# Matrix memory of a hybrid decoder: sample tokens by heads on partition groups, spreads and state updates in split parts

## What is computed

```
F = cumsum(fc);  Dlog = F[t] - F[s] + i[s] (s <= t);  inter = m + F
m_t = max(max_s Dlog, inter);  W = exp(Dlog - m_t);  g = exp(inter - m_t)
S = (q k^T) * W
num = S v + g * (q C);   den = sum(S) + g * (q n)
h = num / max(|den|, exp(-m_t))
C_new = gC * C + sum_s wk[s] k[s] v[s]^T     (wk, gC: from the chunk's last token)
n_new = gC * n + sum_s wk[s] k[s]
```

## Time and profile before

| | |
|---|---|
| median of 3 runs | 1681.45 us |
| the profiled execution, its own time | 1674.11 us |
| its span, first to last instruction | 1672.0 us |
| TensorE busy | 1590.9 us (95%) |
| VectorE, ScalarE, POOL busy | 779.8 (47%), 464.9 (28%), 415.9 (25%) |
| granted TensorE clock, mean | 0.983 |
| chain that ended last | TensorE 52%: L1623 30%, L1601 15%, L1404 6% |

### The profile page before, as it was taken

One profiled execution on the slowest core, in us unless ns is written; L12 is line 12 of the kernel. 1 busy time (PEld: TensorE's weight loads), 2 busy tenths in 40 slices (PEclk: granted clock), 3 DMA queues, 4 the chain that ended last, 5 costly groups with the idle time before them and its releaser, 6 DMA issues.

```text
span 1672.0 us, 27426 instructions
## 1 busy us (share of the span) xinstructions
PE 1590.9 (95%) x10756; PEld 1472.2 (88%) x10756; DVE 779.8 (47%) x1682; ACT 464.9 (28%) x948; POOL 415.9 (25%) x388
## 2 busy tenths in 40 slices
PE   6999999999999998789999999999999999999984
PEld 6986799999996665578789999999999999999983
DVE  2008599999816652454554313223133231332347
ACT  3336523212226562253252111111111111111013
POOL 3520155222200001115394112221122211222004
PEclk8999999999999998999999999999999999999997
DMA  5220231133216107024202111101111011110002
GB/s 168 59 60 15 64 99 56 52 95 98 70 48 232 34 20 228 27 78 159 76 1 76 51 51 51 52 26 51 52 51 51 27 51 51 51 51 26 26 1 104
DMA packets 116781, 110.38 MB, mean 66 GB/s; under 512 B 15906, under 2 KB 101542, under 8 KB 116658
## 3 DMA queue, kind: packets, MB, share of 16 engines
q1 hardware_dynamic: 116658, 108.61, 20.7%
HBM read 88.61 MB, written 19.95 MB: 65 GB/s over the span
## 4 chain that ended last, share of the span: by engine, by line
PE 52%; DVE 2%; issue 1%; ACT 0%; DVEq 0%
PE bank L1623 30%; PE bank L1601 15%; PE bank L1404 6%; DVE y_tm L1835 1%; DVE stats L1810 1%; PE bank L1544 0%; DVE y_tm L1838 0%; PE bank L1767 0%; DVE y_acc L1609 0%; PE bank L1031 0%; PE bank L1000 0%; PE bank L1038 0%; ACT y_tm L1785 0%; DVE moments L1816 0%; DVE moments L1827 0%
## 5 line engine op out<-in xcount | busy, mean ns | idle before, releaser
L1623 PE MATMUL bank<-x_split,gate_up_split 128*128 128x352 f32 x3168 | 510.8, 323 | 2.8 <-issue 1.5
L1623 PEld LDWEIGHTS bank<-x_split,gate_up_split 128*128 128x128 f32 x3168 | 507.3, 188 | 3.7 <-issue 2.1
L2082 PE MATMUL bank<-w_split,xT_split 128*128 128x256 f32 (+1 forms) x2160 | 273.8, 285 | 8.4 <-POOL w_split L2288 8.0
L2082 PEld LDWEIGHTS bank<-w_split,xT_split 128*128 128x128 f32 (+1 forms) x2160 | 258.9, 181 | 14.5 <-issue 9.1
L1601 PE MATMUL bank<-hidden_split,weight_split 128*128 128x352 f32 x1584 | 258.6, 324 | 9.0 <-DVE y_acc L1609 6.9
L1601 PEld LDWEIGHTS bank<-hidden_split,weight_split 128*128 128x128 f32 x1584 | 255.6, 189 | 10.2 <-DVE y_acc L1609 7.8
L1694 DVE TENSOR_TENSOR hidden<-silu,bank 128x352 f32<-128x352 f32 x66 | 34.4, 522 | 413.0 <-ACT silu L1664 412.9
L1729 POOL TENSOR_TENSOR gate_up_split<-gate_up,gate_up_split 128x2048 fp32r<-128x2048 f32 x22 | 104.3, 4739 | 379.0 <-ACT gate_up_split L1656 379.0
L1609 DVE TENSOR_TENSOR y_acc<-y_acc,bank 128x352 f32<-128x352 f32 x264 | 137.3, 521 | 108.9 <-PE bank L1601 107.6
L2380 DVE TENSOR_SCALAR_CACHE_REDUCE chosen<-scores,level 128x384 uint8<-128x384 f32 (+2 forms) x198 | 174.3, 942 | 1.2
L2140 PE MATMUL bank<-xT_split,w_split 128*128 128x352 f32 x864 | 138.8, 323 | 1.2 <-ACT feature_stage L2253 1.2
(11 more groups left out here) (256 smaller groups left out, 1586.0 us busy)
## 6 DMA issues: line engine op xcount, KB each, us to landing
w_unit<-in_w_in_dram SPq DMA_DIRECT2D x16, 1024.0 KB, 5.6
gate_up<-in_w_gate_dram SPq DMA_DIRECT2D x22, 512.0 KB, 4.0
gate_up<-in_w_up_dram SPq DMA_DIRECT2D x22, 512.0 KB, 5.3
down_weight<-in_w_down_dram SPq DMA_DIRECT2D x11, 1024.0 KB, 4.9
scratch_dram<-feature_stage SPq DMA_DIRECT2D x36, 176.0 KB, 1.9
scores<-in_x_prompt_dram SPq DMA_DIRECT2D x8, 512.0 KB, 5.2
out_dram<-stage SPq DMA_DIRECT2D x32, 128.0 KB, 1.7
out_weight<-in_w_out_dram SPq DMA_DIRECT2D x16, 256.0 KB, 6.4
```

The costliest lines, as they stand in the source:

```text
L1623: mm = pe.matmul(PS[2 * c + w][:, 0:CH], gs[u][:, a, w, k, :], xs[:, b, k, c * CH:(c + 1) * CH], start=(k == 0 and (a, b) == PARTS[0]), st ...
L2082: mm = pe.matmul(bank[0:rows(i), 0:HALF], xs1[:, a, k, tile_cols(i)], w[:, b, k, :], start=(k == 0 and (a, b) == PARTS[0]), stop=(k == KD ...
```

## The change

- *Split rows.* Both rows of the spreads are kept as high and low parts in f32r: ScalarE rounds (`act_rows_high`, first thing in its sample attention), POOL subtracts (`pool_rows_low`), SP sends both parts onto partitions 4 to 11 beside the row itself (`sp_samples`, four DMAs), and VectorE casts the three parts to f32r (`dve_rows_round`, ahead of `norm(0)`). A spread is then one f32r matmul. Copies of `head_row` and of the sample mask are loaded early, five DMAs ahead of `load_w(3)`.
- *Heads on partition groups.* In chunk 0 head h has partitions 32h to 32h + 31: scores, weights, `weigh`, outputs, denominator and turning back handle one tile for all four heads; the output matmuls go to four column groups by `tile_position`, sequence by sequence. The wait for the state load (`c_in`) moves from `act_columns` to `sample_outputs`.
- *Split sample updates.* Keys (weighted, three parts on 96 partitions) and values (unweighted, three parts) are f32r; the pieces go to banks 6, 6 and 7.
- *Decay by POOL.* POOL multiplies a head's states by their decays (`scale`); VectorE adds the bank in three sums (`carry_samples`).
- Loads of the sample values: three parts (`mv3`) and one by head (`mvs`).

The core of the diff:

```diff
+            for part in (1, 2):
+                sp.dma_start(head_row[MH * part:MH * part + MH], c_rows[:, T:T + MH * P].rearrange("q (h n) -> q h n", h=MH))\
+                    .then_inc(rows_split, 16)
+            for part in range(1, MH):
+                sp.dma_start(new_mask_t[SMP * part:SMP * part + SMP, :], c_small[0:SMP, 96:128]).then_inc(rows_split, 16)
...
+            sp.wait_ge(pool_made, ROWS_LOW)
+            for w in range(2):
+                for part, src in ((1, rows_high), (2, rows_low)):
+                    sp.dma_start(row_parts[w][MH * part:MH * part + MH, :], src[:, w, :].bitcast(F32)).then_inc(rows_split, 16)
             sp.wait_ge(smp_kT, PAGES * EARLY)
...
+            for h in range(MH):
+                sp.dma_start(mvs[SMP * h:SMP * h + SMP, 0:P], mv_dram[SEQ:T, P * h:P * h + P]).then_inc(c_in, 16)
             for h in range(MH):
                 sp.dma_start(cn[:, h, :, 0:P], state_C[0, :, h].rearrange("b d e -> d b e")).then_inc(c_in, 16)
...
+        def act_rows_high(act):
+            act.wait_ge(rows_split, 16 * 5)
+            act.activation(head2[:, 0:MH, :], head_row, ACT.Copy)
...
+            for w, row in enumerate((b_row, g_row)):
+                act.activation(rows_high[:, w, :], row, ACT.Copy).then_inc(row_act, 1)
+
+        def dve_rows_round(dve):
+            dve.wait_ge(rows_split, 16 * 9)
+            for w in range(2):
+                dve.tensor_copy(row_split[w], row_parts[w]).then_inc(row_step, 1)
...
+            act.wait_ge(mv_loaded, 16 * (LAST + 3))
+            act.activation(v3[0:R3], mv3[0:R3], ACT.Copy).then_inc(sample_split, 1)
+            act.wait_ge(smp_values, 1)
             act.wait_ge(a_turned, 1)
-            act.wait_ge(c_in, 16 * MH)
...
-                pe.matmul(spread_bank(n), head_row[:, h, :], (b_full, g_full)[part][:, 512 * j:512 * j + 512],
+                pe.matmul(spread_bank(n), head2[:, h, :], row_split[part][:, 512 * j:512 * j + 512],
                           start=True, stop=True).then_inc(spread_ps, 1)
...
+            def sample_outputs():
+                pe.wait_ge(st_done, 1)
+                pe.wait_ge(c_in, 16 * 2 * MH)
+                for h in range(MH):
+                    at = SMP * h
+                    pe.matmul(PS[4][at:at + SMP, 0:VE], st[at:at + SMP, 0, 0, 0:SMP], mvs[at:at + SMP, :],
+                              start=True, stop=False, skip_group_check=True, tile_position=(at, at))
+                pe.wait_ge(a_put, 1)
+                for b in range(NB):
                     for h in range(MH):
+                        at = SMP * h
+                        mm = pe.matmul(PS[4][at:at + SMP, 0:VE], qblk[:, h, SMP * b:SMP * b + SMP], cn[:, h, b, :],
+                                       start=False, stop=(b == NB - 1), skip_group_check=True, tile_position=(0, at))
+                mm.then_inc(o_ps, 2)
+
+            def sample_updates(h, j):
+
+                lo, hi, bank = US[j]
+                pe.wait_ge(pool_made, V_BY_SAMPLE[h])
...
+                pe.matmul(PS[bank][:, 0:(hi - lo) * VS], kts3[0:R3, h, :],
+                          vblk[h % 2][0:R3, lo:hi, :].rearrange("p b n -> p (b n)"), start=True, stop=True).then_inc(us_ps, 1)
...
+            def by_sample(h):
                 if h >= 2:
+                    pool.wait_ge(us_ps, 3 * (h - 1))
+                pool.tensor_tensor(vblk[h % 2][0:R3, :, 0:P], v3[0:R3, h, :].bitcast(F32).unsqueeze(1).to_broadcast([R3, NB, P]),
+                                   own[0:R3, :].unsqueeze(2).to_broadcast([R3, NB, P]), ALU.mult).then_inc(pool_made, 1)
+
+            def scale(h):
+                pool.tensor_tensor(cn[:, h], cn[:, h], gls[:, h, :].unsqueeze(2).to_broadcast([P, NB, VE]), ALU.mult)\
+                    .then_inc(pool_made, 1)
+
+            pool.wait_ge(sample_split, 2)
+            by_sample(0)
+            by_sample(1)
+            pool.wait_ge(o_ps, 2)
+            scale(0)
+            scale(1)
+            for h in (2, 3):
+                by_sample(h)
+                scale(h)
...
             def carry_samples(h, j):
+                lo, hi, bank = US[j]
+                x = cn[:, h, lo:hi, :]
+                dve.wait_ge(us_ps, 3 * h + j + 1)
+                dve.wait_ge(pool_made, CN_SCALED[h])
+                dve.tensor_tensor(x, PS[bank][:, 0:(hi - lo) * VS].rearrange("p (b n) -> p b n", n=VS)[:, :, 0:VE], x, ALU.add)\
+                    .then_inc(cn_done, 1)
```

More of the change, by code:

```diff
@@ L764, in dve_samples @@
             pages(1)
+            dve_rows_round(dve)
             norm(0)
@@ L812, in build @@
         b_row = b_full[0:MH, :]
+        row_parts = (b_full, g_full)
+        row_split = (put("b_split", kiT_at, T, F32R), put("g_split", gates_at + T, T, F32R))
+        rows_high, rows_low = (put(f"rows_{part}", iqT_at + 2 * T * n, 2 * T, F32R)[0:MH, :].rearrange("p (w t) -> p w t", w=2)
+                               for n, part in enumerate(("high", "low")))
+        wts = wt[:, 0, SEQ:T]
+        mvs = put("mv_by_head", scd_at + 2 * MH * VE, VE)
+        assert scd_at + (2 * MH + 1) * VE <= gates_at
+        v3 = put("mv_split", stage_at, 512, F32R).rearrange("p (h n) -> p h n", h=MH)
+        kts3 = put("mk_split", stage_at + 512, 512, F32R).rearrange("p (h n) -> p h n", h=MH)
+        w_row = put("sample_weight_row", stage_at + 1696, R3)[0:MH, :]
+        US = [(0, 3, 6), (3, 6, 6), (6, 8, 7)]
         m_row = put("m_row", stage_at + 512, T)[0:MH, :]
@@ new lines, in spread_samples, with sample_scores @@
+                pe.matmul(PS[7][:, P:P + SMP], head2[:, MH, :], row_split[0][:, SEQ:T],
+                          start=True, stop=True, skip_group_check=True).then_inc(spread_ps, 1)
+            def sample_scores():
+                pe.wait_ge(spread_taken, SPREADS)
+                for h in range(MH):
+                    at = SMP * h
+                    mm = pe.matmul(PS[0][at:at + SMP, 0:SMP], mkT[:, h, SEQ:T], mq[:, h, SEQ:T],
+                                   start=True, stop=True, skip_group_check=True, tile_position=(0, at))
+                mm.then_inc(s_ps, 1)
@@ L1061, in pe_mlstm @@
                     spread(spread_no(part, h, 0), part, h, 0)
-            scores(0)
-            keys(0)
-            for e in range(2):
-                outputs(0, e)
+            sample_scores()
+            sample_keys()
+            pe.wait_ge(mv_loaded, 16 * (LAST + 3))
+            pe.wait_ge(pool_made, ONES_SET)
+            sample_outputs()
             for n in range(CK):
@@ L1250, in denominator @@
                 first, both, inv = (den[0:r, n % 2, k] for k in range(3))
+                if c == LAST:
+                    d, em = PS[4][:, P:VE], emcol[:, c, 0:1]
+                    first, both, inv = (den[:, 0, k, 0, 0:1] for k in range(3))
                 dve.scalar_tensor_tensor(out=first, in0=d, scalar=-1.0, in1=em, op0=ALU.mult, op1=ALU.max)\
```

236 lines of the change are left out of this document (139 added, 97 removed).

## The result

The changed kernel takes 1655.1 us in the median of four executions (1652.37 to 1657.58), the kernel before, beside it on the same chip, 1682.18 us (1681.18 to 1683.38): 27 us less, a ratio of 0.984, 95% interval 0.982 to 0.986. A second set of runs gave 1654.46 against 1678.29 us, 0.986 (0.984 to 0.988). The forecast was 1656.5 us against a median of 1681.45.

What follows compares the result with a forecast made beforehand. TensorE alone bounds it from 758 us on; before that, the loop is a ring of waits, 12.0 us a turn. +1.9 + 3.7 - 16.8 - 13.8 = -25.0: 1656.5 us against the median 1681.45, range 1649 to 1667.

Steps and rivals of the forecast that it cites:

- The forecast case: The prediction's main case, given 70%: a shift of -25.0 us, to 1656.5 us against the median.
- the ring of waits: Loop turn where VectorE and ScalarE wait for each other and no engine is full: 12.0 us, predicted 7.4.
- Start: Five small loads on SP's queue ahead of the fourth weight unit: +1.9 us, ends 0 and 2.4.
- All three move together: At the start, SP's unit issue, ScalarE's wait for it and TensorE's wait all shift alike, by 1.9 us.
- Row parts: Landing and casts of the split rows hold VectorE ahead of `norm(0)`: +3.7 us, ends 2.4 and 6.2.
- Columns: Last copy to the second `weigh`: 37.2 us becomes 20.4, so -16.8; ends 18 and 25.
- Turns: Three loop turns of 7.4 instead of 12.0 us: -13.8 us; ends 7.0 and 8.9 a turn.
- The bad ends of the four terms: Slow limits of start, row parts, columns and turns, given together as a shift of -14 us.
- the slow end of the range: Upper limit of the forecast time for the whole kernel: 1667 us.
- Outputs one after another: Rival, 10%: column groups of the sample outputs don't overlap, 10.6 instead of 4.7 us: -19, 1662.5 us.
- POOL and VectorE in turns: Rival, 8%: POOL's scaling blocks VectorE in the loop, turns of 11.2 us: -13.6, 1668 us.
- POOL as the bound: Rival, 2%: POOL's operations before the last head's sums become too slow, from 7.6 us each: +14, 1695.5 us.

Runs made afterwards that it cites:

- a3: Changed kernel with VectorE's two casts of the row parts and the mask column moved behind the first output turn: 1650.65 us, 0.985 of the kernel before.
- c1: Changed kernel with row spreads in f32 over all 128 partitions, as in the kernel before, instead of split rows: 1656.51 us, 0.986 of the kernel before.
- a4: Changed kernel with the five loads behind the fourth weight unit and the casts behind the first output turn: 1650.49 us, 0.983 of the kernel before.
- b4: Same two moves as a4, plus VectorE's wait for the gate rows moved to the gating that reads them: 1647.35 us, 0.982 of the kernel before.
- b1: Changed kernel with the 64 sample output passes ordered head after head: 1660.29 us, 0.989 of the kernel before.

## Why the prediction was right, and where its sizes were off

The forecast case happened: the outputs of the heads overlap, the ring of waits is shorter, POOL's scaling is covered. The time lies within 1.4 us of the number. That closeness is in part luck. A shift of -25.0 was predicted; the medians give -27.1 and -23.8, and the stages, in the means of two profiles, -20.4: the two losses are 6.0 us larger than predicted, the gains 3.4 larger, and 1.9 stand behind the loop, where the prediction had nothing.

*Start, +1.9 predicted, about +6 measured.* The issue of the five was right, 1.89 us. What failed is "All three move together": SP issued the unit 2.8 us later (0.8 of this stood ahead of the five, in the start and the issuing of the index pages), ScalarE had it 4.2 later, TensorE moved by 4.16 (99.99 to 95.83), and behind the longer hole the clock fell, which no term held (0.88 in the window, 1.00 in the same window before). From there it carries to the end of the stage, since TensorE is nearly full, as the prediction said.

*Row parts, +3.7 predicted, +5.4 measured.* The time of the landing came out: 645.5 us plus the 8.4 us by which everything was then late is 653.9, and VectorE went on at 653.97. That too was partly luck: SP took 2.6 us to issue the four parts (1.6 taken), and the last then landed in 1.8 (2.7 taken). The casts were oversized (1.3 us together, predicted 2.3). So the hold itself was smaller than predicted: counted from the first key page `norm(0)` came 2.7 us later than before, in both profiles. The other half of the 5.4 is a term that was missing, again the clock: TensorE stood for 4.77 us and then ran at 0.57, with the 32 score passes in 3.64 us where a3 takes 1.93. The prediction speaks of three parts; the products' 0/1 rows are zero for the first, so a spread adds two.

*Columns, -16.8 predicted, -17.1 in the first profiles and -19.1 in the means.* Right for the reasons given. From the last copy (671.23) to the second `weigh` there are 20.1 us, predicted 20.4. The outputs took 0.66 and 2.81 us and the keys 1.54, 5.0 together at a mean clock of 0.66, where 4.7 had been taken for a clock between the two levels; at 1.00 (c1) they take 3.4, where 3.0 had been taken. The ends of the range were real: a4 and b4 show the gate rows and the state as the next waits once the last copy is 7 to 12 us sooner.

*Turns, -13.8 predicted, -14.2 and -14.9.* Turns of 6.91, 7.46 and 7.47 us; 7.4 had been taken.

*Slips in the sums.* The bad ends of the four terms add up to -12.9, not -14, so the slow end of the range should have been 1668.6. Eight f32 passes in 3.60 us are 0.45 each, not 0.43. Neither changes the argument.

*How far the cause is shown.* The runs took back the order of the outputs (4 us of the columns), the split rows (3.4 to 4.7 us of the columns, 2.0 of the turns) and POOL's decay (some 2 us of the turns). The larger part of both gains was not taken back by a run: the heads in one tile, the state's wait moved behind the scores, the updates in f32r through banks 6 and 7 instead of 7 alone. For it the rows before and after are the evidence: ScalarE's 8.18 us for the state are gone, its wait for the denominator fell from 8.48 to 3.94 us, VectorE's sums follow without idle time.

*Rivals.* Outputs one after another: b1 shows what that costs in this kernel, 4 us of passes and 5 to 6 of time. POOL and VectorE in turns: sums of 387 columns take 0.55 us beside POOL and alone, POOL's operations 1.9 us. The rule of the Trainium skill, page "SBUF — State Buffer", section "SBUF: two separate sides", by which sums with one input in PSUM are not blocked, agrees with these rows. A form with two inputs in SBUF stands in every trace, that of the kernel before too, just behind the loop: there VectorE subtracts two SBUF tiles, 0.64 us an operation with POOL idle (two in 1.27), and one of them takes 1.78 us beside POOL doing the same.

```profile
742.47 9.90 POOL L1566 TENSOR_TENSOR x_split<-mixT,x_split 128x512 fp32r<-128x512 f32 x8 [3.09 <-ACT x_split L1558]
...
744.31 1.78 DVE L1566 TENSOR_TENSOR x_split<-mixT,x_split 128x512 fp32r<-128x512 f32 x1
...
754.16 1.27 DVE L1566 TENSOR_TENSOR x_split<-mixT,x_split 128x512 fp32r<-128x512 f32 x2
```

That agrees with the other half of the rule; no run took it apart further. POOL as the bound: its last scaling is done 8.4 us early. What was not listed as a rival is what came nearest to changing the sum: a short wait that lowers the clock of the work behind it.

## What to carry to other kernels

Price a wait ahead of a full TensorE twice: its own length, and the windows behind it at the lower clock; here two waits that grew by 3.5 and 3.7 us, to 4.8 and 5.0, went with stages longer by 5.4 and about 6. When a part of a change needs data from elsewhere, look for the place in the engine's list where the consumer is still far away: the split rows were worth nothing with the casts ahead of the softmax and some 5 us in the version with the casts behind it (and the other moves). And put products for different column groups next to each other, not group after group.

## What was not expected of the hardware

With f32 spreads over 4 partitions TensorE was busy without a break through 14 us of passes and the granted clock stayed at 0.50; with the same passes over 128 partitions it rose to 0.84 in the mean of such a window, and the second eight ran at 3.60 us. The two runs differ also in what the rows held (zeros in the first), and which of the two it was is open. In the loop the clock fell in some executions and not in others: its third turn takes 7.47 us at 1.00 in the changed kernel and 9.09 at 0.81 in b1, with the same instructions. Why is open.
